# All norms but the first on token columns, matmuls over hi and lo together in the middle of the kernel, and loads put at other units

## What is computed

```python
# first block
mod = silu(c) @ ada_w + ada_b                  # six vectors: sh1, sc1, g1, sh2, sc2, g2
h = rmsnorm(x, norm1_g) * (1 + sc1) + sh1
x = x + g1 * token_mixer(h)                    # h @ w_in, three attentions, recurrence, proj_a, proj_b, w_out
h = rmsnorm(x, norm2_g) * (1 + sc2) + sh2
x = x + g2 * conv_glu_ffn(h)                   # (gelu(conv(gate)) * val) @ ffn_down
x = rmsnorm(x, final_g)
# second block
h = rms_norm(x, norm_w)
q, k, v, a_gate, u, z, g_a, g_s = split(h @ w_in_2)
q, k = rms_norm(q per head of 64), rms_norm(k per head of 64)
# sliding window attention, state space model, gated products, projections
x = x + merged @ w_out_2
```

## Time and profile before

| | us |
|---|---|
| median of 3 runs (lowest to highest) | 2693.28 (2691.06 to 2696.19) |
| the profiled execution | 2692.64 |
| its span, first to last instruction | 2690.9 |
| PE busy in the span | 2597.1 |
| DVE busy | 1877.7 |
| ACT busy | 1107.6 |
| mean granted PE clock | 0.984 |

### The profile page before, as it was taken

One profiled execution on the slowest core, in us unless ns is written; L12 is line 12 of the kernel. 1 busy time (PEld: TensorE's weight loads), 2 busy tenths in 40 slices (PEclk: granted clock), 3 DMA queues, 4 the chain that ended last, 5 costly groups with the idle time before them and its releaser, 6 DMA issues.

```text
span 2690.9 us, 48148 instructions
## 1 busy us (share of the span) xinstructions
PE 2597.1 (97%) x20256; PEld 2505.2 (93%) x20256; DVE 1877.7 (70%) x2519; ACT 1107.6 (41%) x1381; POOL 227.3 (8%) x190
## 2 busy tenths in 40 slices
PE   7999999989999999899999999999999999999999
PEld 5789999889999999899999999999999888899999
DVE  7865667676866674679976556654487898898563
ACT  1033456455333344444443344444444444534432
POOL 0000000000000001000466610001100000000000
PEclk9988999999999999999999999999999999999999
DMA  9974466456888886478866766665555554465664
GB/s 404 424 269 151 156 204 188 142 157 212 274 268 275 278 276 211 134 254 274 278 225 212 221 211 181 183 185 180 165 181 180 157 162 132 149 189 176 195 197 134
DMA packets 243462, 568.13 MB, mean 211 GB/s; under 512 B 17424, under 2 KB 21520, under 8 KB 228784
## 3 DMA queue, kind: packets, MB, share of 16 engines
q1 hardware_dynamic: 233776, 530.33, 60.9%
q0 software_dynamic: 9472, 34.74, 3.6%
HBM read 550.85 MB, written 14.16 MB: 210 GB/s over the span
## 4 chain that ended last, share of the span: by engine, by line
PE 75%; DVE 12%; DVEq 4%; DMA 3%; ACT 3%; issue 2%; SPq 0%; ACTq 0%; POOL 0%
PE pair L1792 65%; DVE wlo L1272 4%; DMA wraw<-ada_wT_dram 3%; ACT whi L1267 2%; DVE wraw L1248 1%; PE pair L1365 1%; PE bank L499 1%; PE pair L1798 1%; DVEq L338 1%; PE pair L1785 1%; PE states_in L684 1%; PE bank L1365 1%; PE states_in L1370 1%; PE states_in L1097 0%; PE pair L1803 0%
## 5 line engine op out<-in xcount | busy, mean ns | idle before, releaser
L1272 DVE TENSOR_TENSOR wlo<-wraw,whi 128x1024 fp32r<-128x1024 f32 x777 | 977.6, 1267 | 586.0 <-ACT whi L1267 559.5
L1267 ACT ACTIVATE whi<-wraw 128x1024 fp32r<-128x1024 f32 x777 | 813.4, 1057 | 1163.9 <-PE pair L1792 669.7
L1792 PE MATMUL pair<-h_hi,whi 128*128 128x256 f32 x3936 | 1136.3, 289 | 22.2 <-DVE h_lo L426 9.2
L1792 PE MATMUL pair<-h_lo,whi 128*128 128x256 f32 x3936 | 1121.5, 285 | 0.0
L1792 PE MATMUL pair<-h_hi,wlo 128*128 128x256 f32 x3936 | 1120.8, 285 | 0.0
L1792 PEld LDWEIGHTS pair<-h_hi,whi 128*128 128x128 f32 x3936 | 763.6, 194 | 41.5 <-issue 34.9
L1792 PEld LDWEIGHTS pair<-h_lo,whi 128*128 128x128 f32 x3936 | 763.9, 194 | 0.6
L1792 PEld LDWEIGHTS pair<-h_hi,wlo 128*128 128x128 f32 x3936 | 763.1, 194 | 0.0
L1248 DVE SCALAR_TENSOR_TENSOR wraw<-wraw,cb 128x2048 f32<-128x2048 f32 x96 | 221.4, 2309 | 58.1 <-DMA wraw<-ada_wT_dram 56.8
L1792 PE MATMUL pair<-hid_hi,whi 128*128 128x256 f32 x768 | 218.5, 284 | 0.0
L1792 PE MATMUL pair<-hid_hi,wlo 128*128 128x256 f32 x768 | 217.3, 283 | 0.0
(11 more groups left out here) (443 smaller groups left out, 3296.5 us busy)
## 6 DMA issues: line engine op xcount, KB each, us to landing
wraw<-w_in_dram SPq DMA_DIRECT2D x312, 512.0 KB, 3.7
wraw<-ada_wT_dram SPq DMA_DIRECT2D x96, 1024.0 KB, 5.8
wraw<-ffn_up_dram SPq DMA_DIRECT2D x192, 512.0 KB, 3.7
wraw<-ffn_down_dram SPq DMA_DIRECT2D x96, 512.0 KB, 4.6
wraw<-w_out_dram SPq DMA_DIRECT2D x64, 512.0 KB, 4.6
wfour<-w_in_dram SPq DMA_DIRECT2D x16, 1024.0 KB, 13.5
wraw<-proj_a_dram SPq DMA_DIRECT2D x32, 512.0 KB, 5.3
wraw<-proj_b_dram SPq DMA_DIRECT2D x32, 512.0 KB, 4.9
```

The costliest lines, as they stand in the source:

```text
L1267: sc.activation(whi[:, r, 0:w], wraw[:, PLACE[z], 0:w], ACT.Copy).then_inc(hi_ready, 1)
L1272: ve.tensor_tensor(wlo[:, PLACE[z], 0:w], wraw[:, PLACE[z], 0:w], whi[:, r, 0:w].bitcast(F32), ALU.subtract).then_inc(lo_ready, 1)
L1792: ins = te.matmul(pair[:, o, :], w[:, at_w + o * P:at_w + (o + 1) * P], x, start=(k == 0 and o % 2 == 0 and t == 0), stop=(k == last and t ...
```

## The change

1. **Wide groups.** PSUM is laid out as two tiles `wides` of four banks; `pairs` and `bank` are parts of them. From `pb 0` to `down 3` of the first half, except `wout`, and for `gate` and `val` of the second half, a unit makes for each output tile one matmul of `whi` on hi and lo side by side (512 columns) and one of `wlo` on hi (256 columns). The two halves are added when the group is emptied: ACT copies the one half to a buffer `tl`, DVE adds the other from PSUM, and the rest of `evac` reads `tl`. The activation pairs are stored with hi and lo of a chunk next to each other.
2. **Norms on tokens.** The sums of `norm2`, `last_norms` and `head_norm` are made with the squares as weights and one column of `ones` (two of `halves`), so that tokens stand on the partitions: 2, 4, 16 or 8 columns in all. Root and reciprocal work on these; DVE widens them, and float32 matmuls with the identity spread them over all partitions into PSUM, where the later instructions read them. A `Sqrt` on one column stands ahead of the squares of the last rows.
3. **Loads.** `ada` rows leave `k 1` and `v 1` (four of them) for a second place in each `lx`. The last 16 leave `gate` and `val` 1 to 4 (two per group) for `wout` (four) and one in each of the twelve `gate` and `val` of the first half. The first `turns` and `bz` loads move from `states` to a job of their own 2 units after the start of `q2 0`, `bz` ahead of `turns`.
4. **Smaller.** The last rows of the recurrence stay in `lr` instead of going to `ob_f`; `ctmp` moves.

```diff
-    at = [(out[of(kind, 1)], s) for kind in ("k", "v") for s in (1, 3)]
-    at += [(out[of("q", i)], 1) for i in range(4)] + [(out[of(kind, i)], 1) for i in range(4) for kind in ("lx", "ly")]
+    at = [(out[of("q", i)], 1) for i in range(4)] + [(out[of("ly", i)], 1) for i in range(4)]
+    at += [(out[of("lx", i)], s) for i in range(4) for s in (1, 3)]
...
-    at = [(out[of(kind, i)], s) for i in range(1, 5) for kind in ("gate", "val") for s in (1, 3)]
+    at = [(out[of("wout", i)], s) for i, s in ((0, 1), (0, 3), (1, 1), (2, 1))]
+    at += [(out[of(kind, i)], 2) for i in range(6) for kind in ("gate", "val")]
...
+    for g in range(of("pb", 0), of("down", 3, 0) + 1):
+        out[g].wide = out[g].kind != "wout"
+    for g in range(of("gate", 0, 1), of("val", 5, 1) + 1):
+        out[g].wide = True
...
+    wides = [ctx.enter_context(nc.psum_tensor(f"banks{n}", [P, 4, 2, T], F32)) for n in range(2)]
+    pairs = [w[:, 0:2, :, :].rearrange("p b c t -> p (b c) t") for w in wides]
+    bank = [wides[n // 2][:, 2 + n % 2, :, :] for n in range(4)]
...
+    def token_sums(acc, x, start=False, stop=False):
+        for b in range(2):
+            ins = te.matmul(acc[:, b:b + 1], x[:, b * P:(b + 1) * P], ones[:, 0:1], start=start and b == 0, stop=stop,
+                            skip_group_check=True)
+        return ins
...
+    def spread(j, out, wide):
+        j.take("to_pe", "pe", wide)
+        if me == "pe":
+            for b in range(2):
+                ins = te.matmul(out[:, b * P:(b + 1) * P], buf[:, b * P:(b + 1) * P], ident[:, :], start=True, stop=True)
+        return j.give("pe_to_dve", "pe", ins)
...
     def head_norm(j, kind, i):
...
-                ins = te.matmul(bank[c // 2][:, c % 2, :], halves[:, :], t1[:, c, :], start=True, stop=True)
+                for b in range(2):
+                    at = 4 * c + 2 * b
+                    ins = te.matmul(bank[0][:, 0, at:at + 2], t1[:, c, b * P:(b + 1) * P], halves[:, 0:P:64], start=True, stop=True)
...
-                ve.reciprocal(t2[:, c, :], t2[:, c, :])
+            ve.reciprocal(hroot[:, 0:w], hroot[:, 0:w])
+            ve.drain()
+            ins = ve.tensor_copy(t1[:, 0:n, :].rearrange("p c (h r) -> p (c h) r", r=64),
+                                 hroot[:, 0:w].unsqueeze(2).broadcast_to([P, w, 64]))
+        yield from j.hand("to_pe", "dve", "pe", ins)
+        if me == "pe":
+            for c in range(n):
+                for b in range(2):
+                    ins = te.matmul(bank[c // 2][:, c % 2, b * P:(b + 1) * P], t1[:, c, b * P:(b + 1) * P], ident[:, :],
+                                    start=True, stop=True)
+        yield from j.hand("pe_to_dve", "pe", "dve", ins)
...
+    job(first_turns, start_of("q2", 0) + 2)
...
+        if gr.wide:
+            e, w = tl, wides[g % 2]
+            yield from j.hand("to_act", "dve", "act", j.drained())
+            if computed("act"):
+                ins = sc.activation(tl[:, :, :], w[:, :, 1, :], ACT.Copy)
+            yield from j.hand("act_to_dve", "act", "dve", ins)
+            if me == "dve":
+                done(ve.tensor_tensor(tl[:, :, :], w[:, :, 0, :], tl[:, :, :], ALU.add))
+                ve.drain()
...
+                if gr.wide:
+                    for o in range(4):
+                        out, cols = wides[g % 2][:, o, :, :], slice(at_w + o * P, at_w + (o + 1) * P)
+                        te.matmul(out, wh[:, cols], X[gr.x][2][:, k, :, :], start=(k == 0), stop=(k == last),
+                                  skip_group_check=True)
+                        ins = te.matmul(out[:, 0, :], wl[:, cols], hi[:, k, :], start=False, stop=(k == last),
+                                        skip_group_check=True)
```

More of the change, by code:

```diff
@@ L50, in __init__ @@
         self.flush = False
+        self.wide = False
 def groups():
@@ L1448, in evac @@
         elif k == "pa":
-            if me == "dve":
+            if GR[of("ga", i)].wide:
+                j.take("act_to_dve", "dve", j.ready["ga"])
+            elif me == "dve":
                 j.eng.wait_ge(*evacuated("ga", i))
@@ L1565, in norm2 @@
         me, ins = j.me, None
-        j.sync("pe_to_dve", "pe", "dve", te.drain() if me == "pe" else None)
+        j.take("pe_to_dve", "dve", j.ready["sums"])
         if me == "dve":
-            ins = ve.tensor_scalar(rstd[:, :], bank[0][:, 0, :], 1.0 / D, EPS, ALU.mult, ALU.add)
+            ins = ve.tensor_scalar(roots[:, 0:2], bank[0][:, 0, 0:2], 1.0 / D, EPS, ALU.mult, ALU.add)
         j.sync("to_act", "dve", "act", ins)
         if me == "act":
-            ins = sc.activation(rstd[:, :], rstd[:, :], ACT.Sqrt)
+            ins = sc.activation(roots[:, 0:2], roots[:, 0:2], ACT.Sqrt)
         j.sync("act_to_dve", "act", "dve", ins)
         if me == "dve":
-            ve.reciprocal(rstd[:, :], rstd[:, :])
+            ve.reciprocal(roots[:, 0:2], roots[:, 0:2])
             ve.drain()
+        j.take("pe_to_dve", "dve", spread(j, SPREAD["h2"][:, 0, :], widened(j, roots[:, 0:2])))
         normed_first(j, "h2")
@@ L1590, in last_norms @@
         if me == "act":
-            ins = sc.activation(rs2[:, :, :], rs2[:, :, :], ACT.Sqrt)
+            ins = sc.activation(roots, roots, ACT.Sqrt)
         j.sync("act_to_dve", "act", "dve", ins)
         if me == "dve":
-            ve.reciprocal(rs2[:, 1, :], rs2[:, 1, :])
+            ve.reciprocal(roots, roots)
             ve.drain()
+        j.take("pe_to_dve", "dve", spread(j, SPREAD["h3"][:, 0, :], widened(j, roots[:, 2:4])))
         normed_first(j, "h3")
@@ L1600, in first_out @@
         me, ins = j.me, None
-        if me == "dve":
-            ve.reciprocal(rs2[:, 0, :], rs2[:, 0, :])
-            ve.drain()
+        v = widened(j, roots[:, 0:2])
+        yield
+        yield
+        v = spread(j, SPREAD["h3"][:, 1, :], v)
+        yield
+        j.take("pe_to_dve", "dve", v)
         for b in range(4):
```

107 lines of the change are left out of this document (61 added, 46 removed).

## The result

The changed kernel takes 2664.57 us, median of 5 executions (2658.78 to 2674.61); the kernel before 2693.65 us beside it (5, 2691.06 to 2696.19). The ratio is 0.9892, 95% interval 0.9871 to 0.9914: faster, by 29 us. The forecast was 54 us, and 2664.57 lies above the top of the range, 2660. The profiled execution of after took 2666.61 us, its span is 2664.9.

A forecast was written before the change was run, and what follows sets the result against it. PE was taken as the bound, busy 2597.1 of 2690.9 us, plus its waits. Terms summed to -54.3 us, -36.0 from wide groups: from 2692.6 to 2638.3, forecast as a median of 2639 us, range 2627 to 2660.

The forecast's parts named there:

- Wide groups, the 346.7 ns: `pb 0` to `down` of half 0, `gate`/`val` of both halves: tile 360.1 to 346.7 ns, 344 units, 36.8 us saved.
- The rule of 2.5 ns per matmul: Rival for the wide groups: only 2.5 ns saved per matmul, 6.9 us instead of 36.8, 2669 us; chance 0.04.
- Wide groups, the emptying "at nothing": Edges of 37 wide groups: extra ACT copy (1.03 us) and DVE add (1.22 us) cost nothing; DVE goes from 83% to 81%.
- the emptying becomes PE's wait: Rival at each wide group's edge: splits queue behind DVE held for ACT's copy, 83 us lost, 2722 us; chance 0.03.
- `ada` rows out of `gate` and `val`, -2.0: Around 1310 us: two waits for splits should go with one row per group, -2.0 us (ends -2.6 and +2).
- `norm2` -1.0, `last_norms` -1.8: First DVE instruction to first normed row: `norm2` 2.73 to 1.7 us, `last_norms` 3.79 to 2.0; ends -4 and +1.
- First `bz` and `turns`, -6.1: Around 2035 us: the 3.1 us wait for `bz` goes, with 3.0 of lowered clock; ends -3.1 and -6.8.
- first `q` and `k`: Where PE is full, the new spread costs 1.8 us for `q`, 0.9 for `k`; +3.1 with `first_out`'s 0.4.
- Second `head_norm` -4.0: Second q: the 5.3 us attention wait and 1.7 of clock go, spread and copy cost 1.8 and 1.2; ends -7 and +2.
- `lx` +2.5: Four `ada` rows moved into `lx` meet attention jobs where PE already waits for DVE: +2.5 us, ends 0 and 9.2.
- `k 1` and `v 1`, -9.0: Without their `ada` rows, two waits go and the first compression product runs at full clock: -9.0 us, ends -12 and -2.
- The rival that the clock would still fall there: Early compression product: -2.4 instead of -9.0, and moved rows cost +9 instead of +2.5; 2652 us, chance 0.25.

The follow-up runs named there:

- a_again: The changed kernel run once more without an edit, for its spread and tile steps: 2667.53 us (4 executions, ratio 0.9898).
- micro_steps: Not the kernel: TensorE alone streams float32r matmuls in several orders and pauses; old order 360.0 ns per tile, the 512/256 pair 353.3 in 11 stretches, 346.7 in 3.

## Why VectorE fell behind

DVE's timeline of after, ahead of the longest of the waits (PE's last matmul starts at 1334.94; the wait of 3.8 us ends with the split that starts at 1337.63):

```profile
1321.78 2.30 DVE L1329 TENSOR_TENSOR wlo<-wraw,whi 128x1024 fp32r<-128x1024 f32 x1
1324.00 1.21 DVE L1477 TENSOR_TENSOR tl<-banks,tl 128x1024 f32<-128x1024 f32 x1
...
1328.41 2.10 DVE L1329 TENSOR_TENSOR wlo<-wraw,whi 128x1024 fp32r<-128x1024 f32 x1 [1.78 <-ACT whi L1324]
1330.43 7.08 DVE L838 SCALAR_TENSOR_TENSOR t<-tl,vec,t 128x255 f32<-128x255 f32 x8
1337.63 1.23 DVE L1329 TENSOR_TENSOR wlo<-wraw,whi 128x1024 fp32r<-128x1024 f32 x1
```

The same eight steps of the convolution in the kernel before, which read the product in PSUM:

```profile
1330.06 3.37 DVE L797 SCALAR_TENSOR_TENSOR t<-pair,vec,t 128x255 f32<-128x255 f32 x8
```

Same work, 7.08 us in place of 3.37. The change has the wide group's sum written to `tl` in SBUF, and the convolution now reads both its operands in SBUF. Without GpSimd at work, 1130 to 1290 us, it costs nothing: 13.32 us for 32 instructions, 0.42 each. From 1293.5 on GpSimd makes the rotation tables, and single instructions of the convolution take up to 1509 ns. The splits are slowed beside it too, in both kernels: 2.30 and 2.10 us above where others take 1.23, and in the kernel before two of them take 4.30 us from 1323.83 on.

**a_late.** GpSimd's work elsewhere:

```diff
-    job(make_turns, end_of("val", 3), end_of("val", 3) + 2)
-    job(output_factors, start_of("gate", 2, 1), end_of("val", 3, 1))
+    job(make_turns, start_of("down", 0), start_of("down", 0) + 2)
+    job(output_factors, start_of("gate", 4, 1), end_of("val", 5, 1))
```

> The kernel after with two pieces of work that run on GpSimd and VectorE moved later: make_turns from the end of val 3 (half 0) to the start of down 0, output_factors from gate 2..val 3 of half 1 to gate 4..val 5 of half 1. Theory C1, contention: the convolutions (8 to 24 operations with both operands in SBUF, 0.68 us each for 24 in 16.30 us while GpSimd works, against 0.41 us for 9.90 us before, when one operand was in PSUM) and the splits of wlo (1.56 us beside GpSimd, 1.18 without) are slow because GpSimd works beside them, VectorE falls behind, and TensorE waits for the splits 5 times between 1277 and 1386 us (0.9 to 3.8 us each, about 10 us together with the clock behind them). By it the waits of that stretch vanish or move behind the start of down 0, the 24 operations take about 10 us, and gate/val of half 1 ends about 5 to 8 us earlier; the whole is 2657 to 2662 us. Theory C2, load alone: VectorE is too full with wide groups (97.3 of 105 us busy), whoever works beside it; then the waits stay, moved by at most some us, and the time is the after kernel's (2666.5) within 2 us. If the moved work collides in down 0 with the splits there, the gain of half 1 is given back: 2665 to 2669.

**a_psum.** The sum back into PSUM:

```diff
-            e, w = tl, wides[g % 2]
+            w = wides[g % 2]
+            e = w[:, :, 0, :] if k == "gate" else tl
...
-                done(ve.tensor_tensor(tl[:, :, :], w[:, :, 0, :], tl[:, :, :], ALU.add))
+                ins = ve.tensor_tensor(e[:, :, :], w[:, :, 0, :], tl[:, :, :], ALU.add)
+                if k != "gate":
+                    done(ins)
```

> The kernel after, with the sum of the two halves of a gate group's wide product written back into PSUM instead of into SBUF, and the convolution reading it there. Nothing else changes; PSUM is set free after the convolution instead of before it. Theory C1 (an operation of VectorE with both operands in SBUF is slowed while GpSimd works, one with an operand in PSUM is not): the 24 operations of a gate group beside GpSimd go from 16.3 us to 9.9 us, the waits of TensorE at 1277 to 1386 us go or shrink to under 3 us together, and the time is 2658 to 2663. Theory C3 (the operations are slow because of what VectorE itself does around them, the waits come from splits that stand behind long groups): the 24 take 14 to 17 us still and the time stays at 2665 to 2668. A cost that could hide either: the next but one group of the same PSUM buffer waits for the convolution; a gate group's PE work is 22.4 us and the buffer's next use is two groups later, so it should not show; if it does, a wait of TensorE at a group's first matmul appears and the time goes up by 1 to 5 us.

The convolution's line in a_again (unchanged), a_psum and a_late, 1290 to 1400 us: duration ns min/median/max.

```profile
L838 DVE SCALAR_TENSOR_TENSOR t<-tl,vec,t x16: 470/1278/1601, 1322.5 to 1378.3; 128x255 f32<-128x255 f32 x8, 128x254 f32<-128x254 f32 x8
```

```profile
L838 DVE SCALAR_TENSOR_TENSOR t<-banks,vec,t x16: 469/473/481, 1321.5 to 1369.7; 128x255 f32<-128x255 f32 x8, 128x254 f32<-128x254 f32 x8
```

```profile
L838 DVE SCALAR_TENSOR_TENSOR t<-tl,vec,t x16: 477/480/485, 1318.7 to 1363.6; 128x255 f32<-128x255 f32 x8, 128x254 f32<-128x254 f32 x8
```

Each of the two cures takes the median from 1278 to 473 and 480 ns. a_late: 2657.16 us (4, ratio 0.9862, 0.9847 to 0.9877), no wait for a split over 0.15 us in `gate/val`, that stage 277.1 us in place of 287.9 (some 2 of the 10.8 are the pair's step, at 346.7 ns from 1285 us on in its trace). `make_turns` has instructions of GpSimd alone, so up to 1371 us, where it now starts, nothing but GpSimd's work is missing. Nor is the load given back in `down`: 133.1 us in place of 135.0. a_psum: 2656.58 us (4, 0.9864, 0.9842 to 0.9886; expected 2658 to 2663), four short waits for splits left, 3.6 us together, and one of 0.7. In a_psum the splits still meet GpSimd, which the cure doesn't touch. C1 holds; that DVE is too full whoever works beside it (C2) and that DVE's own order is at fault (C3) fall.

**ports** measures the slowing by itself:

```diff
+ for beside in [0, 12, 0, 24]:        # operations of GpSimd beside this round
+     4 x scalar_tensor_tensor(acc, tl, vec, acc)      # L50, both operands in SBUF
+     4 x scalar_tensor_tensor(acc, bank, vec, acc)    # L54, one in PSUM
+     3 x tensor_tensor(wlo, raw, whi, subtract)       # L58
+     3 x tensor_copy(wlo, raw)                        # L61
```

> A kernel of its own (its output is not the reference's): VectorE does, four times over, 4 multiply-adds of 255 columns with both operands in SBUF, 4 with one operand in PSUM, 3 subtractions of 1024 columns with both operands in SBUF (as the splits of wlo) and 3 copies of 1024 columns with one operand; in the 2nd and the 4th of the four, GpSimd multiplies tiles of 512 columns beside it. Theory C1 (two operands in SBUF are slowed by GpSimd, others are not): alone 0.40 to 0.45 us, 0.40 to 0.45, 1.1 to 1.3 and 0.6 to 1.2; beside GpSimd the first goes to 0.7 to 1.5 us and the third to 1.6 us or more, the second stays. Theory C4 (GpSimd slows every operation that touches SBUF at all): the second and the copies become slower too, by a like factor. Theory C3 (GpSimd does not slow VectorE; in the kernel it is DMA or ScalarE): all four phases are equal.

DVE's timeline in `ports`, first round alone, second beside GpSimd:

```profile
6.43 2.17 DVE L50 SCALAR_TENSOR_TENSOR acc<-tl,vec,acc 128x255 f32<-128x255 f32 x4
8.68 2.16 DVE L54 SCALAR_TENSOR_TENSOR acc<-bank,vec,acc 128x255 f32<-128x255 f32 x4
10.91 3.83 DVE L58 TENSOR_TENSOR wlo<-raw,whi 128x1024 fp32r<-128x1024 f32 x3
14.81 2.23 DVE L61 CAST wlo<-raw 128x1024 fp32r<-128x1024 f32 x3
17.21 4.85 DVE L50 SCALAR_TENSOR_TENSOR acc<-tl,vec,acc 128x255 f32<-128x255 f32 x4 [0.17 <-issue]
22.13 2.16 DVE L54 SCALAR_TENSOR_TENSOR acc<-bank,vec,acc 128x255 f32<-128x255 f32 x4
24.36 6.00 DVE L58 TENSOR_TENSOR wlo<-raw,whi 128x1024 fp32r<-128x1024 f32 x3
30.43 4.26 DVE L61 CAST wlo<-raw 128x1024 fp32r<-128x1024 f32 x3
```

Two operands in SBUF: 2.17 to 4.85 us. One in PSUM: 2.16 and 2.16. The split's subtraction: 3.83 to 6.00. The copy, with one operand in SBUF and none in PSUM, is slowed too, 2.23 to 4.26, so my C1 was too narrow; C3 falls, and so does C4, by the row that doesn't move. GpSimd's twelve operations lasted until 34.1 us, over all of the second round. Rounds three and four repeat the numbers within 0.01 us. The Trainium skill, "GPSIMD Engine Reference", section "8. Key points", says that GpSimd shares its SBUF interfaces with VectorE and contends with instructions that have two SBUF inputs or run in a 2-port mode. The rows with two SBUF inputs agree, 2.17 to 4.85 us. Whether the copy, at 1.4 columns per ns, runs in such a mode, no run here shows. I had that rule to hand for the prediction and didn't look at where the operands would lie.

## The moved rows and loads

**a_headold, a_wout12, a_noturns** each put one part of the change back:

```diff
# a_headold
-    at = [(out[of("q", i)], 1) for i in range(4)] + [(out[of("ly", i)], 1) for i in range(4)]
-    at += [(out[of("lx", i)], s) for i in range(4) for s in (1, 3)]
+    at = [(out[of(kind, 1)], s) for kind in ("k", "v") for s in (1, 3)]
+    at += [(out[of("q", i)], 1) for i in range(4)] + [(out[of(kind, i)], 1) for i in range(4) for kind in ("lx", "ly")]
# a_wout12
-    at = [(out[of("wout", i)], s) for i, s in ((0, 1), (0, 3), (1, 1), (2, 1))]
+    at = [(out[of("wout", i)], s) for i, s in ((1, 1), (1, 3), (2, 1), (2, 3))]
# a_noturns
-    job(first_turns, start_of("q2", 0) + 2)
+        for _ in first_turns(j):     # at the start of states
+            pass
```

> The kernel after, with the ada rows (the small extra matmuls that carry the modulation) of the first stage back in k 1 and v 1 (steps 1 and 3) and lx 2 and 3 with one each, as before. My recorded sum gives the move of these rows -9.0 us in k 1 and v 1 and +2.5 in lx, 6.5 net. Theory H1, the sum's: the time goes up by 5 to 8 us over the after kernel's 2666.5, to 2672 to 2674, and the stretch from the first h1 unit to the start of q is again about 8 us longer. Theory H2: the shorter early stretch (212.3 us after, 220.6 before) comes from another edit of the change (the compression product without its wait, the clock at full); then the time stays within 2 us of 2666.5.

Measured: 2681.17 us (4, ratio 0.9954, 0.9938 to 0.9971), 13.6 more than a_again and 16.6 more than after. The chain that ended last, 160 to 245 us, of a_headold:

```profile
159.73 2.30 DVE wraw L1305 x2
...
168.31 2.97 DVEq L349
171.32 13.91 PE banks L539 x64
...
234.26 7.09 PE banks L539 x64
```

It is the earlier trace rows again, to the last digit of the two products. In after both run at full clock:

```profile
169.16 7.09 PE banks L539 x64
...
225.87 7.09 PE banks L539 x64
```

From the first unit of `h1` to `q 0` a_headold needs 80.4 us, before 80.0, and the twelve other profiled executions here, which have the rows moved, 67.9 to 70.3. So these rows are worth 10.1 to 12.6 us there, and H1's mechanism holds. Behind it, from `q 0` to `pa 0`, where the `lx` groups and their rows stand, a_headold needs 454.5 us, before 455.0, after 455.6, and the twelve 453.9 to 458.1, in the median 456.0: the rows in `lx` cost 1 to 1.5 us, less than that stage varies. The time, 2681.17, lies above H1's 2672 to 2674 all the same. A part of that is the pair's step: in the profiled execution `gate/val` of half 1 was at 353.3 ns, 271.4 us, where after and a_again had 266.2. (An `ada` row is a load and one instruction of VectorE, not the matmuls that my expectation names.)

> The kernel after, with the four ada rows of the wout groups at groups 1 and 2 (two each, as before) instead of two in group 0. wout with the second norm took 103.6 us before, 107.4 after, 106.8 and 104.1 in two variants. Theory W1: two ada rows in group 0 together with their loads make the load of w_out late (ScalarE waited 9.4 us for it, the squares came late, a wait of 2.48 us at 1024.93 us and half clock behind it); with them moved back the wait vanishes and the stretch is 103 to 104 us, the whole 2662 to 2665. Theory W2: the lateness is that of the transfers and of the wide groups' fuller engines ahead of wout, not of the rows; the stretch stays at 106 to 107.5 us, and the whole at 2666 to 2668.

Measured: 2663.72 us (4, 0.9886, 0.9871 to 0.9901). The wait of 2.5 us is gone, and the stages `pa 0` to `norm2` are 421.8 us, 5.4 less than after's 427.2 (`norm2` 65.8 for 67.4). a_three and a_three_again below, with the rows at the same place, need 421.8 too; after, a_again, a_late, a_psum, a_headold and a_noturns 424.4 to 427.2. W1 holds in the traces, for 2.6 to 5.4 us; the median lies 0.9 under after's and 3.8 under a_again's, which alone would settle nothing.

> The kernel after, with the first bz and turns loads issued at the start of the states job again, as before. My recorded sum gives their move -6.1 us (the wait of 3.1 us for bz and 3.0 us of the half clock behind it), ends -3.1 and -6.8. If right: this kernel is 2672 to 2674, with a wait of about 3 us for bz near 2010 us and a mean clock of 0.6 to 0.75 in the 10 us around it. If the next thing was late anyway (the states job waits for something else by then), the time stays at 2666 to 2668.

Measured: 2661.92 us (4, 0.9886, 0.987 to 0.9901), no slower than after. The wait is back, but small:

```profile
PE banks L1149 <- DMA bz<-B_dram: 1.3, 1, 1.3
```

The clock stays at 1.00 in 2000 to 2050 us. My expectation was wrong: in the kernel before the same wait was 3.1 us and the clock fell behind it. The likely reason, argued and not shown: the first `q` and the `k` now cost PE 3 us more, so PE reaches the wait later and the load has had its time. From `q2` to the first product with `bz` a_noturns needs 84.9 us, after 83.5: of the 6.1 this move holds the small wait, 1.3, and the other edits have the rest.

## The step, once the waits are gone

**a_three** takes both cures and a_wout12's rows.

> The kernel after with three of the edits together: the gate groups' sums in PSUM, make_turns and output_factors later, the wout ada rows in groups 1 and 2. Alone they gave -9.9 us, -9.4 us and -2.8 us against 2666.5. The first two take away the same waits, so they do not add up. If waits are all there is: 2654 to 2657. If the fuller VectorE also costs where no wait shows (the step of the pair of matmuls that begins after a pause, 353.3 or 346.7 ns), the time depends on how the stretches fall: with all 344 wide units at 346.7 ns, 2648; with all at 353.3, 2660.

Measured: 2657.19 us (4, ratio 0.986, 0.9843 to 0.9876), no better than either cure alone. Its profile has no wait for a split in `gate/val`, and `gate/val` of half 1 at 271.3 us and `down` of half 0 at 135.7: 353.3 ns in nearly all wide units, 344 x 8 x 6.7 ns = 18.3 us over 346.7. The forecast stood 2657 - 2639 = 18 us under it. A part is elsewhere: from the first unit of `h1` to `pa 0` it needs 528.4 us, the longest of the kernels with the moved rows (522.2 to 528.4). Whether the step is really worth 18 us in the kernel was open; four more runs asked.

> TensorE alone, as in micro_steps (its output is not the reference's), now with longer runs of one width: pair (512, 256, ...), four and four, eight and eight, sixteen and sixteen, each in 6 stretches after pauses of different lengths and, but for the pair, in 2 without a pause; then 256 columns alone and 512 columns alone. Theory S1, the change of width costs: a matmul of 512 columns is 226.7 ns and one of 256 is 120.0 in a run of its own, 346.7 per tile, and each step from one width to the other adds some ns. Four and four measured 351.3, so 18.5 ns for one run of each; then eight and eight is 346.7 + 18.5 / 8 = 349.0 per tile, sixteen and sixteen 347.9, and the two do not depend on the pause. Theory S2, the level is drawn at the start for any order: then eight and eight also lies at 346.7 in some stretches and at 353.3 in others.

`micro_runs`, PE's timeline with eight and eight, behind a pause:

```profile
243.92 1.11 PE L82 MATMUL banks<-x,wl 128*128 128x256 f32 x8
244.87 2.00 PE L79 MATMUL banks<-x,wh 128*128 128x512 f32 x8
246.72 1.12 PE L82 MATMUL banks<-x,wl 128*128 128x256 f32 x8
247.67 2.00 PE L79 MATMUL banks<-x,wh 128*128 128x512 f32 x8
```

247.67 - 244.87 = 2.80 us for eight tiles. Read over all eight stretches, with and without a pause, it is 2.79, behind the first round: 349 ns per tile, and no stretch at another level. Sixteen and sixteen gave 5.57 us, 347.9. Four and four gave 350.0 in two of eight stretches and 350.9 in six. The pair drew again: three of six stretches at 353.3, three at 346.7. So S1 holds for eight and sixteen: beside the 346.7 ns per tile of equal widths, a round of two changes of width costs 20 ns, however long. With four the round costs 13 to 17 ns, and the pair's 6.7 or 0: there the level counts, as S2 has it.

> The same kernel as a_three, for comparison on the same chip. Its profile had 353.3 ns per pair in nearly all of the 344 wide units, 344 x 8 x 6.7 = 18.3 us over what 346.7 would give, and no wait for splits in gate/val. Expected 2655 to 2660; by the start's draw of the step (theory A) some stretches may lie at 346.7, each of 96 units worth 5.1 us.

> a_three with four matmuls of 512 columns and then four of 256. S1: 351.3 ns per tile everywhere, 344 x 8 x 2.0 = 5.5 us less than all at 353.3: 2651 to 2653 where a_three is 2657. S3, the time won on TensorE is lost again in waits for splits, as DVE sets the pace: within 2 us of a_three.

> a_three with all eight matmuls of 512 columns of a unit and then its eight of 256. S1: 349.0 ns per tile everywhere, 344 x 8 x 4.3 = 11.8 us less than all at 353.3: 2644 to 2647 where a_three is 2657, and units every 2.79 us in the profile. S2: units of 2.773 or 2.827 us by stretch, and a time between 2640 and 2658. S3, VectorE sets the pace: within 3 us of a_three, with waits for splits at the edges of gate/val groups.

```diff
# a_eight, beside a_three's edits
+            if gr.wide:
+                tiles = [(2 * n + kk, wides[g % 2][:, o, :, :], slice(kk * CB + o * P, kk * CB + (o + 1) * P))
+                         for kk in range(2) for o in range(4)]
+                for k, out, cols in tiles:
+                    te.matmul(out, wh[:, cols], X[gr.x][2][:, k, :, :], start=(k == 0), stop=(k == last), ...)
+                for k, out, cols in tiles:
+                    ins = te.matmul(out[:, 0, :], wl[:, cols], hi[:, k, :], start=False, stop=(k == last), ...)
```

Measured on one chip, with the same before (2693.77 us, 9 executions):

```
kernel          median (lowest to highest), n      ratio, 95% interval       gate/val half 1   down half 0
a_three_again   2654.32 (2648.61 to 2657.35), 5    0.9848, 0.9834 to 0.9861        271.4 us      135.7 us
a_three_four    2650.03 (2647.25 to 2656.34), 4    0.9840, 0.9826 to 0.9853        269.4         134.7
a_eight         2648.96 (2641.19 to 2651.17), 4    0.9827, 0.9812 to 0.9843        268.2         134.1
```

a_eight, PE's timeline in `gate/val` of half 1, units every 2.79 us:

```profile
1600.94 1.11 PE L1879 MATMUL banks<-h,wlo 128*128 128x256 f32 x8
1601.89 2.00 PE L1876 MATMUL banks<-h,whi 128*128 128x512 f32 x8
1603.73 1.12 PE L1879 MATMUL banks<-h,wlo 128*128 128x256 f32 x8
```

The stages fall as S1 says: 96 units by 271.4 - 268.2 = 3.2 us, 96 x 8 x 4.3 ns = 3.3. PE does not wait for the splits instead (one wait, 1.1 us, in a_three_again one of 1.2), so S3 falls. In the whole the medians differ by 5.4 us where S1 gave 11.8, and the two intervals overlap, so the whole does not show the gain by itself; executions of one kernel differ by up to 10 us, and a_three_again's lowest, 2648.61, fits stretches drawn at 346.7 (96 units 5.1 us), though only the profiled execution of each can be read. (In that one a_three_again had 346.7 from 1116 to 1254 us.) a_eight beats before by 1.7% and has the lowest time of all that ran.

## Why the prediction was wrong

Point by point, by its own steps:

- **Wide groups, the 346.7 ns.** The step that failed first: "An output tile of one chunk therefore goes from 360.1 to 226.7 + 120.05 = 346.7 ns". Both prices were right for runs of one width, and `micro_runs` measured them so. The change alternates the widths, of which no row of before spoke. What the runs showed in its place: the pair comes at 346.7 or 353.3 ns; after had 200 of 344 units at the dearer one, 10.7 us. My own mark against it, "350 ns or more", was the right one to watch. The rule of 2.5 ns per matmul that the prediction cites from the Trainium skill ("TensorE: Matmul & The Clock Gate", section "Wait — 56ns, not 53.3ns?") does not hold for these float32r matmuls: even the dearer runs apart, the cheaper level leaves 346.7 - 320 = 26.7 ns beside the columns of a pair, 13.4 each, and the old order in `micro_steps` 120.0 - 106.7 = 13.3.
- **Wide groups, the emptying "at nothing".** I counted the add and took DVE from 83% to 81%. The count of instructions was right, 82.5% from 1130 to 1300 us; their duration beside GpSimd was not looked at. From 1293.5 us on, GpSimd works, and eight instructions of the convolution with both operands in SBUF take 7.08 us in place of 3.37. DVE is then busy for 101.6 of 110 us (96.9 before), and five waits of PE for splits follow, 8.4 us, with a mean clock of 0.98 over 110 us, some 1.7 us more: together about 10 (2.6 of them stood there before and are the next point's). Of my rivals the fourth, "the emptying becomes PE's wait", had this mechanism, but at every group's edge and for 83 us (with 37 groups; there are 41, so 92); it occurs only beside GpSimd, at a chance that I put at 0.03.
- **`ada` rows out of `gate` and `val`, -2.0.** The old waits around 1310 us (2.1 and 0.5) stayed, for the same reason: with all groups narrow (a_notwide) they are gone, as forecast, and with GpSimd moved (a_late) too. The four rows "meet an idle DVE: 0" in `wout` cost 2.6 to 5.4 us: two in group 0 made the next wait (a_wout12).
- **`norm2` -1.0, `last_norms` -1.8.** The chain from the mean to the first scaled row is 1092.10 - 1089.79 = 2.31 us where the earlier trace rows has 2.73, not 1.7:

```profile
1089.79 0.15 DVE L1643 TENSOR_SCALAR ltmp<-banks 128x2 f32<-128x2 f32 x1
1090.21 0.17 DVE L1649 RECIPROCAL ltmp<-ltmp 128x2 f32<-128x2 f32 x1 [0.27 <-ACT ltmp L1646]
1090.46 0.29 DVE L378 COPY rstd<-ltmp 128x256 f32<-128x256 f32 x1
1092.10 1.86 DVE L440 SCALAR_TENSOR_TENSOR t<-res,scA,banks 128x256 f32<-128x256 f32 x4 [1.34 <-PE banks L387]
```

  The small instructions are as summed; the hand-over to PE and back, 1.34 us of waiting, is what I put at 0.6. PE's pauses there fell from 10.3 to 9.8 us, 0.5 gained; `down` of half 1 with `last_norms` gained 1.1.
- **First `bz` and `turns`, -6.1; first `q` and `k`.** The time is right: the wait is gone, from the first product with `bz` to the second it is 24.3 us for 27.1 as the clock no longer falls, and the 3 us that the spreads cost (2.7 in the sum) ate the wait's 3.1 in the `q2` row. The cause is right in part only: with the loads back in their old place only 1.3 us of it are lost (a_noturns).
- **Second `head_norm` -4.0.** With the 3.0 of the clock behind `bz` the stage should gain 7.0 and gained 9.1, within the ends: the wait of 5.3 is gone with its clock. The other kernels with the same code there need 299.9 to 304.8 us, a gain of 5.6 to 10.5.
- **`lx` +2.5.** +0.6 in after, within the ends and inside the spread of that stage.
- **`k 1` and `v 1`, -9.0.** Right, -10.6, for the reason given: both products in 7.09 us. The rival that the clock would still fall there did not come; that 2652 lies nearer to the result is chance.

The range was wrong since every case but the last two kept the 36 us whole.

## What to carry to other kernels

A price read where instructions of one shape follow each other holds for that order alone: where a change alternates shapes, forecast both levels or measure the alternation, and group equal widths where the accumulation allows it. When a sum says that an engine has room, ask of each of its instructions in which memory the operands lie and who works beside it, not only how many are added; one operand left in PSUM kept the convolution at its pace beside GpSimd. And where a variant wins less than its parts, compare stage by stage: here every stage outside the wide groups came out within 2.3 us of the sum, which put the search where the loss was.

## What was unexpected

- The 512/256 pair has two levels, 353.3 and 346.7 ns, kept for as long as PE is not interrupted (1385.7 to 1784 us in after) and drawn anew behind a pause: in `micro_steps` 11 and 3, in `micro_runs` 3 and 3. In the nine traces of kernels with the pair every change of level follows a pause of PE or a stretch at half clock; a pause of 0.02 us is enough (a_three_again, 1254.15 us). Where the pair starts straight behind 256-column matmuls, without a pause, it was at 353.3 each time: four times in `micro_steps`, and in all nine traces from `pb 0` to `wout`. What decides the draw behind a pause stays open.
- The slowing beside GpSimd: 0.54 to 1.21 us for 255 columns with both operands in SBUF, 1.28 to 2.00 for the subtraction of 1024, 0.74 to 1.42 for the copy of 1024, none with one operand in PSUM.
- Executions of one wide kernel spread wider than those of before: 2658.78 to 2674.61 (five) against 2690.97 to 2698.2 (the kernel before, nine beside a_again). The draw of the step would do this, 344 units being worth 18.3 us between all at one level and all at the other; it was not shown, as each kernel left one trace.
